# A gated four-branch mixer layer on one core: four small edits around the attention, among them half of the softmax normalisation moved from GpSimd to VectorE

## Chip, cores and metric

The kernel runs on 1 core of a Trainium2 chip. The metric is the device time of one execution in microseconds; the time of a kernel is the median of several runs.

## What is computed

One layer works on a sequence of 1024 tokens with 1024 channels, all in float32. A wide projection of x gives the inputs of four branches; each branch ends in a gated product and a projection, the four results are merged, projected by w_out, added to x and layer-normalised. The change touches the forgetting attention (branch C, 8 heads of 64, causal, query blocks of 128) and the stretch behind it, where the memory cross-attention (branch M) starts. Cut to these:

```python
def _forgetting_attention(q, k, v, logf):
    bsz, seq, heads, dh = q.shape
    scale = dh ** -0.5
    cum = jnp.cumsum(logf, axis=1).transpose(0, 2, 1)
    outs = []
    for i in range(seq // Q_BLOCK):
        q0, end = i * Q_BLOCK, (i + 1) * Q_BLOCK
        s = jnp.einsum('bqhd,bkhd->bhqk', q[:, q0:end], k[:, :end]).astype(jnp.float32) * scale
        decay = cum[:, :, q0:end, None] - cum[:, :, None, :end]
        ...
        s = jnp.where(causal, s + decay, -jnp.inf)
        p = jax.nn.softmax(s, axis=-1).astype(v.dtype)
        outs.append(jnp.einsum('bhqk,bkhd->bqhd', p, v[:, :end]))
    return jnp.concatenate(outs, axis=1)

logf = jax.nn.log_sigmoid((c_f + b_forget[l]).astype(jnp.float32))
o_c = _forgetting_attention(q, k, v, logf).reshape(bsz, seq, C_W)
y_c = (o_c * jax.nn.silu(c_gate)) @ p_c[l]
o_m = _cross_attention(m_q, mk, mv)
y_m = (o_m * jax.nn.silu(m_gate)) @ p_m[l]
```

## The kernel before

Every matrix product of float32 data is made of three matmuls: each operand is split into a rounded high part and the rest (hi and lo), and hi x hi, lo x hi and hi x lo are accumulated. ScalarE makes the high parts, GpSimd or VectorE the low ones by subtraction. The order of each engine's work is written out by hand, and engines are tied together by counting semaphores.

**The stages.** Up to about 590 us TensorE works on the wide projection in pairs of column tiles (`product`, L744 to L746). Then come the first tiles of q, k and v, the forget gates and the memory's k and v (595 to 645 us). The attention runs from there to 943 us in four head pairs c = 0 to 3 (`pair`), then the memory attention together with the branch projections, then w_out and the final layer norm.

**The forget gates.** log sigmoid is made on 8 rows of 1024: ScalarE has |z|, exp(-|z|) (L1339) and ln u (L1341) with u = 1 + exp(-|z|); VectorE corrects ln u by a term with 1/u, a RECIPROCAL (L2024), sums it up (`negcum`) and goes on to k_raw, km_lo, q_stack (`q_lo`) and k_stack_lo (`k_lo`). The sums go to DRAM and come back as `bias`. TensorE's first `scores` wait for k_stack_lo.

**A head pair** has 16 units u (2 heads x 8 query blocks; i = u mod 8; a unit has i + 1 key blocks). For each unit:
- TensorE: `scores` (L899, L901) two units ahead; `turn` transposes the normalised probabilities (L916) into one of two banks of `pt`, in one batch or two; `weigh` (L929), once per two units, multiplies them by v_stack. Between these stands the stream: 64 steps of three matmuls per pair (`stream_part`, L815 to L817), four per unit, which project the next pair's q, k, v and the gate.
- VectorE, iteration k: `biased(k + 1)` adds bias and mask to scores and takes minima (L2085, L2089), `turned_lo(k - 1)` makes pT_lo (L2106), `invert(k + 1)` takes the reciprocal of the row sums (L2099); then, in some iterations, q_lo, k_lo, out_add, gate_half.
- ScalarE: pT_hi (L1394), which in even units waits for the last weigh, exp (L1383), high parts of weights (L1220) and of v (L1412).
- GpSimd, iteration k: `diag_bias(k + 2)` (L1646), `normalise(k + 1)` (L1659) scales the probabilities by the reciprocal, `split_w` for k = 0, 4, 8, 12 (L1622), and for k = 2 in pairs 1 to 3 `z_product` (L1679), the previous pair's o times its gate.

In unit 1 `turn_v` also transposes v (L942: 8 transposes, two batches of 4); the second batch goes into the bank that unit 0 used, and waits for pT_lo of unit 0. The probabilities of unit 1 need the first bank back, so `turn` waits for the low part of v_stack (L2126).

**Behind the last pair** TensorE issues mscores(0) and mscores(1), then for w = 0 to 15 nine steps of M_FILL with the memory attention's transposes in between. The last `weigh(3, 7)` stands behind the first five of these steps. Its result is shifted by ScalarE (L1368), added by VectorE (L2051), and on VectorE follow the row maxima and their negation (L2187, L2190), the memory's normalisation (L2197) and za_lo (L2243), which TensorE needs from step 16 on (L832).

## Time and profile before

| what | value |
|---|---|
| median of 3 runs | 1236.19 us (1235.81 to 1237.3) |
| the profiled execution's own time | 1234.27 us |
| its span | 1232.5 us |
| TensorE matmuls busy | 1202.4 us (98%) |
| VectorE busy | 767.5 us (62%) |
| ScalarE busy | 538.6 us (44%) |
| GpSimd busy | 758.7 us (62%) |
| granted TensorE clock, mean | 0.998 |
| chain that ended last | TensorE 84%, VectorE 8%, GpSimd 3% |

The span runs from the first to the last instruction of one execution; 1.8 us of its time lie outside. A row of the timeline reads: start, duration, engine, line, operation, tile written <- tiles read, shapes, count, and in brackets how long the engine had stood still before it and what ended that. A row of the list of waits reads: total, number of times, longest. In the names of the profile DVE is VectorE, ACT is ScalarE, POOL is GpSimd, PE is TensorE. Rows that merge several instructions overlap their neighbours.

### The profile page before, as it was taken

Reading aid. Unit: us, or ns where it says so; the run is one execution under the profiler, and the core shown is the slowest. Engines: PE = TensorE matmul, PEld = TensorE weight load, DVE = VectorE, ACT = ScalarE, POOL = GpSimd, SP = SyncE. Lnnn points to the kernel's source line nnn. Section 1 sums busy time; section 2 is a strip of 40 time slices with the busy share of each in tenths; the row PEclk is TensorE's granted clock in tenths of the full one; section 3 lists DMA queues with packets and bytes.
Section 4 is the critical chain, followed back from the end, with each engine's and each line's share of the span. In section 5 each row is a group of like instructions: output and inputs, shape, how many; then the busy total and the mean of one; then the engine's idle time right before and its main releaser. Section 6 shows DMA issues by size and latency. Waiting matters only on the chain.

```text
span 1232.5 us, 15758 instructions
## 1 busy us (share of the span) xinstructions
PE 1202.4 (98%) x5704; PEld 998.8 (81%) x5704; DVE 767.5 (62%) x1254; ACT 538.6 (44%) x991; POOL 758.7 (62%) x582
## 2 busy tenths in 40 slices
PE   8999999999999999999999999999999999999997
PEld 6888888888888888888878878878788788878886
DVE  5623865676665755347695564565655776876755
ACT  5433424344434444566344655646555443415000
POOL 6677787877876877877128666677664225557000
PEclk9999999999999999999999999999999999999999
DMA  8012131132332332335222011112002433377141
GB/s 275 9 60 69 35 103 55 66 120 104 102 137 103 103 117 89 137 105 187 87 66 55 24 46 52 35 52 52 18 18 86 165 134 112 111 244 248 63 137 69
DMA packets 91277, 118.61 MB, mean 96 GB/s; under 512 B 6072, under 2 KB 72632, under 8 KB 91200
## 3 DMA queue, kind: packets, MB, share of 16 engines
q1 hardware_dynamic: 91200, 117.60, 29.2%
q8 instruction: 46, 0.75, 0.3%
q14 instruction: 31, 0.25, 0.1%
HBM read 92.39 MB, written 25.20 MB: 95 GB/s over the span
## 4 chain that ended last, share of the span: by engine, by line
PE 84%; DVE 8%; POOL 3%; ACT 2%; issue 2%; DMA 1%; DVEq 0%; SPq 0%; ACTq 0%; POOLq 0%
PE pj L744 11%; PE pj L745 11%; PE pj L746 11%; PE pj L816 4%; PE pj L815 4%; PE pj L817 4%; PE pj L1074 4%; PE pt L745 3%; PE pt L746 3%; PE pt L744 3%; PE po L929 3%; PE pt L916 3%; PE pj L832 2%; PE pj L833 2%; PE pj L834 2%
## 5 line engine op out<-in xcount | busy, mean ns | idle before, releaser
L1569 POOL TENSOR_TENSOR ring_lo<-w_pair,ring_hi 128x512 fp32r<-128x512 f32 x168 | 232.5, 1386 | 110.7 <-ACT ring_hi L1130 110.5
L1622 POOL TENSOR_TENSOR w_lo<-w_raw,w_hi 128x128 fp32r<-128x128 f32 (+1 forms) x104 | 105.1, 1031 | 126.5 <-ACT w_hi L1220 124.4
L1659 POOL TENSOR_SCALAR probs<-probs,rinv 128x128 f32<-128x128 f32 (+3 forms) x64 | 126.4, 1975 | 90.8 <-DVE rinv L2099 90.6
L1130 ACT ACTIVATE ring_hi<-w_pair 128x512 fp32r<-128x512 f32 x168 | 105.1, 628 | 160.6 <-PE pj L746 108.6
L1780 DVE SCALAR_TENSOR_TENSOR po<-glu,cwa,po 128x512 f32<-128x512 f32 x232 | 159.4, 747 | 20.6 <-ACT po L1181 20.6
L744 PE MATMUL pj<-t_hi,ring_hi 128*128 128x512 f32 x392 | 152.8, 390 | 0.3 <-DVE slot L1744 0.3
L745 PE MATMUL pj<-t_lo,ring_hi 128*128 128x512 f32 x392 | 152.5, 389 | 0.0
L746 PE MATMUL pj<-t_hi,ring_lo 128*128 128x512 f32 x392 | 152.5, 389 | 0.0
L815 PE MATMUL pj<-xT_hi,w_hi 128*128 128x512 f32 x320 | 126.0, 394 | 0.0
L816 PE MATMUL pj<-xT_lo,w_hi 128*128 128x512 f32 x320 | 125.5, 392 | 0.0
L817 PE MATMUL pj<-xT_hi,w_lo 128*128 128x512 f32 x320 | 125.1, 391 | 0.0
L1744 DVE TENSOR_TENSOR slot<-pj,copy_p 128x512 f32<-128x512 f32 x56 | 38.5, 688 | 85.6 <-PE pj L746 85.4
L744 PE MATMUL pj<-xT_hi,ring_hi 128*128 128x512 f32 x224 | 87.1, 389 | 0.0
L745 PE MATMUL pj<-xT_lo,ring_hi 128*128 128x512 f32 x224 | 87.1, 389 | 0.0
L746 PE MATMUL pj<-xT_hi,ring_lo 128*128 128x512 f32 x224 | 87.1, 389 | 0.0
L744 PEld LDWEIGHTS pj<-t_hi,ring_hi 128*128 128x128 f32 x392 | 73.6, 188 | 16.5 <-DVE slot L1744 1.3
L746 PEld LDWEIGHTS pj<-t_hi,ring_lo 128*128 128x128 f32 x392 | 73.6, 188 | 15.3
L745 PEld LDWEIGHTS pj<-t_lo,ring_hi 128*128 128x128 f32 x392 | 73.6, 188 | 15.1
L1593 POOL TENSOR_TENSOR w_pair<-w_pair 128x512 f32<-128x512 f32 x56 | 81.8, 1461 | 6.2
L2106 DVE TENSOR_TENSOR pT_lo<-pt,pT_hi 128x512 fp32r<-128x512 f32 (+2 forms) x96 | 50.4, 553 | 53.5 <-ACT pT_hi L1394 53.5
L1744 DVE TENSOR_TENSOR slot<-pt,copy_p 128x512 f32<-128x512 f32 x28 | 19.4, 692 | 96.6 <-PE pt L746 96.6
L1138 ACT ACTIVATE copy_p<-pj 128x512 f32<-128x512 f32 x70 | 41.8, 597 | 81.3 <-PE pj L746 81.3
(343 smaller groups left out, 2939.1 us busy)
## 6 DMA issues: line engine op xcount, KB each, us to landing
w_pair<-in_w_in SPq DMA_DIRECT2D x28, 1024.0 KB, 5.3
gate_scratch<-slot SPq DMA_DIRECT2D x16, 1024.0 KB, 4.0
gate<-gate_scratch SPq DMA_DIRECT2D x32, 512.0 KB, 3.8
w_raw<-in_w_in SPq DMA_DIRECT2D x20, 512.0 KB, 3.9
z_scratch<-slot SPq DMA_DIRECT2D x8, 512.0 KB, 2.6
bias<-cum_scratch SPq DMA_DIRECT2D x8, 512.0 KB, 4.2
wout_raw<-in_w_out SPq DMA_DIRECT2D x8, 512.0 KB, 5.7
x_tok<-in_x SPq DMA_DIRECT2D x8, 512.0 KB, 4.4
```

The costliest lines, as they stand in the source:

```text
L744: nc.tensor.matmul(dst, w_h, hi, start=k == 0 and p in (1, 2, 5), stop=False, skip_group_check=True)
L745: nc.tensor.matmul(dst, w_h, lo, start=False, stop=False, skip_group_check=True)
L746: mm = nc.tensor.matmul(dst, w_l, hi, start=False, stop=k == KH - 1, skip_group_check=True)
L815: nc.tensor.matmul(pj[:, bank, :], w_hi[:, j % 2, k, :], hi, start=k == 0, stop=False)
L816: nc.tensor.matmul(pj[:, bank, :], w_hi[:, j % 2, k, :], lo, start=False, stop=False)
L817: mm = nc.tensor.matmul(pj[:, bank, :], w_lo[:, j % 2, k, :], hi, start=False, stop=k == nk - 1)
L1130: nc.scalar.activation(ring_hi[:, j % RING, :, :], w_src(u, p), ACT.Copy).then_inc(s_rhi, 1)
L1569: nc.gpsimd.tensor_tensor(ring_lo[:, j % RING, :, :], w_src(u, p), ring_hi[:, j % RING, :, :], ALU.subtract).then_inc(s_rlo, 1)
L1593: nc.gpsimd.tensor_tensor(dst, in0, in1, op).then_inc(s_sadd, 1)
L1622: nc.gpsimd.tensor_tensor(w_lo[:, j % 2, k, :], w_raw[:, j % 2, k, :], w_hi[:, j % 2, k, :], ALU.subtract).then_inc(s_wlo, 1)
L1659: nc.gpsimd.tensor_scalar(probs[:, u % 2, 0:(i + 1) * P], probs[:, u % 2, 0:(i + 1) * P], rinv[:, u % 2, 0:1], None, ALU.mult).then_inc(s_ ...
L1780: nc.vector.scalar_tensor_tensor(out=acc if n < PAD_A else src, in0=src, scalar=cwa[:, ct, n:n + 1], in1=acc, op0=ALU.mult, op1=ALU.add).t ...
```

## The change

Four edits. (1) ScalarE makes 1/u as exp(-ln u); VectorE's reciprocal goes, and the counts of that chain's semaphores with it. (2) In unit 1 of each pair `turn_v` stands ahead of the unit's stream steps, and three steps instead of two stand ahead of `turn`. (3) `weigh(3, 7)` stands ahead of the first five M_FILL steps. (4) `normalise` on GpSimd returns for odd units; VectorE scales them inside `invert`, behind its own reciprocal, with a semaphore of its own.

```diff
-        s_pn = sem("probs_normalised")
+        s_pn = sem("probs_normalised_even")
+        s_pnv = sem("probs_normalised_odd")
...
-        F_STEPS = 9
+        F_STEPS = 8
...
-                pe.wait_ge(s_pn, UNITS * c + u + 1)
+                pe.wait_ge((s_pn, s_pnv)[u % 2], NT * c + u // 2 + 1)
...
-                    cut = 4 * u + (3 if u == 0 else 2)
+                    cut = 4 * u + (3 if u < 2 else 2)
+                    if u == 1:
+                        turn_v(c)
                     stream_part(s + S_C, S_C, 4 * u, cut)
                     if u == 0 and c:
                         weigh(c - 1, UNITS // 2 - 1)
-                    if u == 1:
-                        turn_v(c)
                     turn(c, u)
...
+            weigh(CT - 1, UNITS // 2 - 1)
             for w in range(2 * NT):
 
                 m_fill(PER * w, PER * w + 5)
-                if w == 0:
-                    weigh(CT - 1, UNITS // 2 - 1)
-                pe.wait_ge(s_pn, UN + w + 1)
+                pe.wait_ge(s_pn, UN // 2 + w + 1)
...
             nc.scalar.activation(f_l[:, :], f_u[:, :], ACT.Ln).then_inc(s_fa, 1)
+            act.wait_ge(s_fa, 6)
+            nc.scalar.activation(f_r[:, :], f_l[:, :], ACT.Exp, scale=-1.0).then_inc(s_fa, 1)
             split_w(1, 0)
...
             def normalise(c, u):
                 un, i = UNITS * c, u % NT
+                if u % 2:
+                    return
                 pool.wait_ge(s_ri, un + u + 1)
...
-            nc.vector.reciprocal(f_r[:, :], f_u[:, :]).then_inc(s_fv, 1)
-            dve.wait_ge(s_fv, 4)
+            dve.wait_ge(s_fv, 3)
+            dve.wait_ge(s_fa, 7)
...
                 nc.vector.reciprocal(rinv[:, u % 2, 0:1], rsum[:, u % 2, 0:1]).then_inc(s_ri, 1)
+                if u % 2:
+                    i = u % NT
+                    dve.wait_ge(s_ri, un + u + 1)
+                    nc.vector.tensor_scalar(probs[:, 1, 0:(i + 1) * P], probs[:, 1, 0:(i + 1) * P],
+                                            rinv[:, 1, 0:1], None, ALU.mult).then_inc(s_pnv, 1)
```

What this does to the order of instructions shows best at three places. On TensorE, in unit 1 of head pair 1, before:

```order
L815 MATMUL pj<-xT_hi,w_hi 128x512
L816 MATMUL pj<-xT_lo,w_hi 128x512
L817 MATMUL pj<-xT_hi,w_lo 128x512
L942 MATMUL pt<-ident,v_raw 128x128 x8
L916 MATMUL pt<-ident,probs 128x128 x2
```

and now, from the v transposes on (lines stand one further down):

```order
L943 MATMUL pt<-ident,v_raw 128x128 x8
L816 MATMUL pj<-xT_hi,w_hi 128x512
L817 MATMUL pj<-xT_lo,w_hi 128x512
L818 MATMUL pj<-xT_hi,w_lo 128x512
L816 MATMUL pj<-xT_hi,w_hi 128x512
L817 MATMUL pj<-xT_lo,w_hi 128x512
L818 MATMUL pj<-xT_hi,w_lo 128x512
L816 MATMUL pj<-xT_hi,w_hi 128x512
L817 MATMUL pj<-xT_lo,w_hi 128x512
L818 MATMUL pj<-xT_hi,w_lo 128x512
L917 MATMUL pt<-ident,probs 128x128 x2
```

Three steps now stand between v's transposes and those of unit 1's probabilities, where none stood. On GpSimd, units 2 to 5 of head pair 1 (384 to 768 columns), before:

```order
L1659 TENSOR_SCALAR probs<-probs,rinv 128x384
L1646 TENSOR_TENSOR bdiag<-bias,maskc 128x128
L1659 TENSOR_SCALAR probs<-probs,rinv 128x512
L1679 TENSOR_TENSOR z_raw<-z_raw,sg 128x1024
L1646 TENSOR_TENSOR bdiag<-bias,maskc 128x128
L1659 TENSOR_SCALAR probs<-probs,rinv 128x640
L1646 TENSOR_TENSOR bdiag<-bias,maskc 128x128
L1659 TENSOR_SCALAR probs<-probs,rinv 128x768
```

and now:

```order
L1664 TENSOR_SCALAR probs<-probs,rinv 128x384
L1648 TENSOR_TENSOR bdiag<-bias,maskc 128x128
L1684 TENSOR_TENSOR z_raw<-z_raw,sg 128x1024
L1648 TENSOR_TENSOR bdiag<-bias,maskc 128x128
L1664 TENSOR_SCALAR probs<-probs,rinv 128x640
L1648 TENSOR_TENSOR bdiag<-bias,maskc 128x128
L1624 TENSOR_TENSOR w_lo<-w_raw,w_hi 128x256
```

The scalings of 512 and 768 columns are gone, and the z product follows that of 384. On ScalarE, in the forget gates, now:

```order
L1339 ACT_TABLE_LOAD
L1339 ACTIVATE f_e<-f_abs 8x1024
L1341 ACT_TABLE_LOAD
L1341 ACTIVATE f_l<-f_u 8x1024
L1343 ACT_TABLE_LOAD
L1343 ACTIVATE f_r<-f_l 8x1024
L1220 ACTIVATE w_hi<-w_raw 128x256
```

A third table load stands ahead of the new exponential; the load that stood ahead of the attention's first exponential (L1383) is no longer there.

## Rows read from the trace of the kernel before

**Rows 1.** Page, busy time of the engines.
```profile
PE 1202.4 (98%) x5704; PEld 998.8 (81%) x5704; DVE 767.5 (62%) x1254; ACT 538.6 (44%) x991; POOL 758.7 (62%) x582
```

**Rows 2.** TensorE's waits over the whole span: total, times, longest.
```profile
PE pt L916 <- DVE v_stack L2126: 4.3, 4, 1.1
PE pt L916 <- DVE pT_lo L2106: 2.9, 16, 0.2
PE pt L916 <- POOL probs L1659: 2.8, 3, 1.0
PE pj L899 <- DVE k_stack_lo L2069: 2.6, 1, 2.6
PE po L832 <- DVE za_lo L2243: 2.2, 2, 1.8
```

**Rows 3.** Timeline of ScalarE, VectorE and TensorE, 610 to 645 us.
```profile
610.82 1.28 ACT L1341 ACT_TABLE_LOAD   x1
619.20 1.06 ACT L1341 ACTIVATE f_l<-f_u 8x1024 f32<-8x1024 f32 x1 [7.10 <-DVE f_u L2019]
620.34 6.53 DVE L2024 RECIPROCAL f_r<-f_u 8x1024 f32<-8x1024 f32 x1
...
640.81 1.65 DVE L2069 TENSOR_TENSOR k_stack_lo<-k_raw,k_stack_hi 64x1024 fp32r<-64x1024 f32 x1
642.51 0.39 PE L899 MATMUL pj<-k_stack_hi,q_stack 128*128 128x256 f32 x1 [2.63 <-DVE k_stack_lo L2069]
```

**Rows 4.** Timeline of VectorE and TensorE, unit 1 of pair 1.
```profile
723.71 0.28 DVE L2106 TENSOR_TENSOR pT_lo<-pt,pT_hi 128x128 fp32r<-128x128 f32 x1
723.74 0.39 PE L815 MATMUL pj<-xT_hi,w_hi 128*128 128x512 f32 x1
...
724.43 1.03 PE L942 MATMUL pt<-ident,v_raw 128*128 128x128 f32 x8
726.53 0.41 PE L916 MATMUL pt<-ident,probs 128*128 128x128 f32 x2 [1.07 <-DVE v_stack L2126]
```

**Rows 5.** Timeline of GpSimd, VectorE, TensorE: units 3, 4 of pair 1; last row unit 12.
```profile
730.95 2.59 POOL L1659 TENSOR_SCALAR probs<-probs,rinv 128x512 f32<-128x512 f32 x1 [1.81 <-DVE rinv L2099]
733.51 2.40 POOL L1679 TENSOR_TENSOR z_raw<-z_raw,sg 128x1024 f32<-128x1024 f32 x1
734.47 0.17 DVE L2099 RECIPROCAL rinv<-rsum 128x1 f32<-128x1 f32 x1 [0.25 <-ACT probs L1383]
739.22 0.77 PE L916 MATMUL pt<-ident,probs 128*128 128x128 f32 x5 [0.95 <-POOL probs L1659]
771.77 2.77 POOL L1659 TENSOR_SCALAR probs<-probs,rinv 128x640 f32<-128x640 f32 x1 [2.18 <-DVE rinv L2099]
```

**Rows 6.** Timeline of VectorE, TensorE and ScalarE behind the last pair.
```profile
942.54 1.29 DVE L2106 TENSOR_TENSOR pT_lo<-pt,pT_hi 128x512 fp32r<-128x512 f32 x2
943.61 0.28 PE L1019 MATMUL pj<-km_lo,q_stack 128*128 128x256 f32 x1
946.09 0.20 ACT L1467 ACTIVATION_READ_ACCUMULATOR probs<-pj,rmin 128x1 f32 x1
949.27 0.38 ACT L1368 ACTIVATE otmp<-po 64x256 f32<-64x256 f32 x1 [2.98 <-PE po L929]
950.86 1.76 DVE L2190 TENSOR_SCALAR rmin<-rmin 128x2 f32<-128x2 f32 x1
```

**Rows 7.** Single lines: duration in ns min/median/max, first and last start.
```profile
L1998 DVE TENSOR_SCALAR mem_sb<-mem_sb,mv,rinv x2: 807/811/815, 599.1 to 599.8; 128x1024 f32<-128x1024 f32 x2
L2197 DVE TENSOR_SCALAR probs<-probs,rinv x32: 343/354/1197, 946.5 to 1062.0; 128x256 f32<-128x256 f32 x32
L2069 DVE TENSOR_TENSOR k_stack_lo<-k_raw,k_stack_hi x16: 1196/1220/2324, 638.7 to 884.8; 64x1024 fp32r<-64x1024 f32 x16
```

**Rows 8.** VectorE's wait for pT_hi in the attention, 640 to 960 us; its shortest.
```profile
DVE pT_lo L2106 <- ACT pT_hi L1394: 53.5, 31, 3.0
...
779.77 0.89 DVE L2106 TENSOR_TENSOR pT_lo<-pt,pT_hi 128x512 fp32r<-128x512 f32 x2 [1.36 <-ACT pT_hi L1394]
```

More of the change, by code:

```diff
@@ L2023, in _ @@
                                            op0=ALU.subtract, op1=ALU.subtract).then_inc(s_fv, 1)
-            nc.vector.reciprocal(f_r[:, :], f_u[:, :]).then_inc(s_fv, 1)
-            dve.wait_ge(s_fv, 4)
+            dve.wait_ge(s_fv, 3)
+            dve.wait_ge(s_fa, 7)
             nc.vector.scalar_tensor_tensor(out=f_e[:, :], in0=f_e[:, :], scalar=-1.0, in1=f_r[:, :],
                                            op0=ALU.mult, op1=ALU.mult).then_inc(s_fv, 1)
-            dve.wait_ge(s_fa, 6)
-            dve.wait_ge(s_fv, 5)
+            dve.wait_ge(s_fv, 4)
             nc.vector.tensor_tensor(f_l[:, :], f_l[:, :], f_e[:, :], ALU.add).then_inc(s_fv, 1)
             nc.vector.tensor_scalar(f_z[:, :], f_z[:, :], -1.0, 0.0, ALU.mult, ALU.max).then_inc(s_fv, 1)
-            dve.wait_ge(s_fv, 7)
+            dve.wait_ge(s_fv, 6)
             nc.vector.tensor_tensor(f_l[:, :], f_l[:, :], f_z[:, :], ALU.add).then_inc(s_fv, 1)
             dve.wait_ge(s_fone, 1)
-            dve.wait_ge(s_fv, 8)
+            dve.wait_ge(s_fv, 7)
             nc.vector.tensor_tensor_scan(negcum[:, :], f_one[:, :], f_l[:, :], 0.0, ALU.mult,
```

## Prediction

> **What bounds the kernel now.** I read the page first: TensorE is busy for 1202.4 of 1232.5 us [rows 1]. So only time in which TensorE stands still can be won, and that is 30.1 us: a lead before the first matmul, a tail after the last one, and the waits between. Next came TensorE's list of waits [rows 2]: 4.3 us for the v stack (4 times), 2.8 us for GpSimd's normalised probabilities (3 times), 2.6 us once for the k stack, 2.2 us for za_lo (2 times), and 2.9 us in 16 small pieces for pT_lo; apart from the lead the list has nothing else above 0.6 us. Then the timeline around each of the first four places [rows 3 to 6] shows what ended last there. VectorE is not the bound: in the attention it waits 53.5 us for pT_hi alone, 31 times [rows 8]. New VectorE work fits in there if it falls at the right moments.
>
> **Repair 1, the reciprocal.** The 8x1024 reciprocal takes 6.53 us, in a chain in which VectorE never rests until k_stack_lo, 1.65 us from 640.81; TensorE starts its first score matmul at 642.51, after a wait of 2.63 us [rows 3]. The change has ScalarE make 1/u as exp(-ln u). The order of instructions shows a table load between the two (the load that stood before the first softmax exponential is gone for it). ln runs from 619.20 for 1.06 us, the load is 1.28 us like the earlier one, exp is 1.06 us like ln, both 8x1024: f_r is there at 619.20 + 1.06 + 1.28 + 1.06 = 622.60 instead of 620.34 + 6.53 = 626.87, which is 4.27 us earlier [rows 3]. VectorE's chain moves by that, and ScalarE (2.34 us more work, under the memory projections) may hold some of it back; 2.63 us is all that TensorE can take, since its own stream then reaches the scores first. Gain 2.6 us; bounds 1.9 us (4.27 less 2.34) and 2.6 us. I take the upper end, because ScalarE waits for TensorE in between and catches up.
>
> **Repair 2, v turned one step earlier.** In unit 1 of each of the four head pairs TensorE issues 8 transposes of v, then waits 1.07 us until VectorE has made v_stack's low part [rows 2, 4]. A stream step is 0.69 us (723.74 to 724.43 in rows 4). The change issues the v transposes right after the first step instead of the third, and has three steps between them and the probabilities' transposes: 2.07 us of cover where there was none. The old wait goes. But the second four v transposes reuse the bank of unit 0, so they need pT_lo of unit 0, done at 723.71 + 0.28 = 723.99 [rows 4]. TensorE would now be there at 724.43 - 2 x 0.69 + half of 1.03 = 723.57. New wait 0.4 us in pairs 1 to 3; in pair 0, where pT_lo was held up by GpSimd's normalisation of unit 1 and is no more, 0.1 us. Gain 4 x 1.07 - 3 x 0.4 - 0.1 = 3.0 us; bounds 1.0 us (if pT_lo is 0.4 us later everywhere, the new wait is 0.8 us) and 4.3 us.
>
> **The normalisation.** GpSimd loses 32 TENSOR_SCALARs, VectorE gets them. Two rows bound their price: 128x256 takes 354 ns, 128x1024 takes 811 ns [rows 7]. With 0.50 and 0.66 us for 512 and 768 columns the eight of a pair cost 2 x (0.35 + 0.50 + 0.66 + 0.81) = 4.6 us, 18.6 us in all. All of that stands behind a reciprocal and ahead of the next unit's bias step on VectorE. I put it on the path with 0 us in the units where VectorE waits for pT_hi next, since the least wait I found ahead of a unit with two batches is 1.36 us [rows 8].
> What it gives: in unit 4 of pairs 1 to 3 TensorE waits 0.95 us [rows 5]. There GpSimd did normalise(3) (2.59 us), z_product (2.40 us), a diagonal and then normalise(4). Without normalise(3) the z product starts up to 2.6 us earlier and is out of the way. Then normalise(4) hangs on its reciprocal: 734.47 + 0.17, plus 2.77 us (its duration when VectorE's k_stack_lo runs beside it, row of 771.77), is 737.4 [rows 5]. TensorE without its wait is there at 739.22 - 0.95 = 738.27, and by repair 2 some 0.65 us earlier, 737.6. The new normalise(3) on VectorE, 0.50 us, stands ahead of that reciprocal. So 0.3 us of wait stays: gain 3 x (0.95 - 0.3) = 2.0 us, bounds 0 and 2.85 us.
> What speaks against it: VectorE is held up by a running GpSimd instruction. A 128x256 scaling took 1197 ns instead of 354 beside GpSimd's split of weights, k_stack_lo took 2324 instead of 1220 ns beside the z product [rows 7], and the 128x2 negation took 1.76 us [rows 6]. The new instruction can be caught by what GpSimd still runs in such a unit: the z product (unit 3, pairs 1 to 3) or a split of weights (units 1, 5, 9 and 13). At the least this costs nothing, where VectorE starts first. At the most it is 2.4 us in one unit (z product, rows 5), less the 1.36 us of rest. I charge 0.1 us a pair and 0.1 us for the z products, 0.5 us together, near the lower end because of the rests in rows 8. The Trainium skill, "SBUF — State Buffer", section "SBUF: two separate sides", speaks against this edit: the two engines share a port pair by an exclusive lock, and the later one waits for the whole instruction of the other. The durations named agree with it; taken for every scaling that meets a split it gives rival D, 1240.2 us, where the rests of rows 8 give 1227.1 us.
>
> **Repair 3, the last weigh.** weigh(3, 7) now runs ahead of five stream steps (3.4 us). It needs the last pT_lo, done at 942.54 + 1.29 = 943.83; TensorE ends the memory scores' issue at about 943.7 (0.12 us behind the matmul of 943.61), so 0.15 us of wait is new [rows 6]. After it stands a single chain: o shifted (949.27), added, row maxima, negation (1.76 us beside the z product, as it will be again), exponential, normalisation, za_lo, for whose third and fourth blocks TensorE waits 2.2 us [rows 2, 6]. weigh now ends 3.3 us earlier, but ScalarE reads the sum of its first memory exponential until 946.29 [rows 6], so the shift starts at 946.3 and the chain moves by 2.5 us or more, which covers the 2.2 us. Gain 2.2 - 0.15 - 0.1 (the fourth block) = 1.95 us; bounds 0 and 2.2 us.
>
> **Sum.** 2.6 + 3.0 + 2.0 - 0.5 + 1.95 = 9.05 us. The profiled execution took 1234.27 us; against its own time that gives 1225.2 us. The median of the three runs is 1.9 us above that execution, and the forecast is for a median: 1236.19 - 9.05 = 1227.1 us. What lies behind this stretch is bound by TensorE and moves as a whole.
>
> **Rivals.**
> A. As above, 1227.1 us; own range 1224.8 to 1229.0. Chance 0.66.
> B. Port trouble and late reciprocals eat part: the wait in unit 4 stays at 0.95 us and each pair loses a further 0.7 us where a scaling stands behind a GpSimd instruction. 9.05 - 2.0 - 2.8 = 4.25 us, 1231.9 us. For it: the longest durations [rows 7]. Against: VectorE's rests [rows 8]. Chance 0.20.
> C. The change does not do what it says: v's transposes only trade one wait for another, since pT_lo of unit 0 is late (repair 2 gives its lower bound, 1.0 us). 1227.1 + 2.0 = 1229.1 us. For it: pT_lo ends 0.4 us behind TensorE already in this trace [rows 4]. Chance 0.08.
> D. Slower. The scaling meets GpSimd's split of weights and delays pT_lo of the even unit before it. In units 5 and 13 of each pair, 8 places, such a split follows on GpSimd, and TensorE already waits 0.18 us for exactly that pT_lo (16 pieces in rows 2, units 7 and 15 are the other 8), so only VectorE's rest of 1.36 us stands between a late VectorE and TensorE. With a scaling of 0.66 us and 2.4 us of blocking each place loses 0.66 + 2.4 - 1.36 = 1.7 us: 1236.19 - 9.55 + 8 x 1.7 = 1240.2 us. It decides from 9.55 / 8 = 1.2 us a place. For it: the longest scaling, 1197 ns [rows 7]. Against: that one lost 0.84 us, not 2.4. Chance 0.04.
> E. The change is worth more than the waits: the small waits of 0.18 us vanish as well, and repair 2 gives its 4.3 us. 1224 us or a little under. Chance 0.02.
>
> **How the numbers follow.** About 0.2%, 2.5 us, is what a measurement of this kernel can tell from no change. A, C and E are faster by more; of B (4.25 us) all but 0.04, of D nothing. Faster 0.92, within 0.2% 0.04, slower 0.04. The range takes A with the bounds of its unknown terms, C, and about half of B: 1224.3 to 1231.5 us.
>
> **What would show it.** Right: TensorE's wait for k_stack_lo gone and an exp of 8x1024 at about 621.6; v_stack gone from TensorE's waits and a wait of about 0.4 us ahead of the second four v transposes; the wait for GpSimd's probs at 0 to 0.4 us a pair; za_lo nearly gone; VectorE's scaling at 0.35 to 0.81 us, GpSimd with 32 scalings fewer. Wrong: scalings on VectorE of 1.5 us and more with a longer wait of TensorE for pT_lo behind them, or a first score matmul that still waits.

## The result, and the profile after

The changed kernel takes 1223.22 us (median of 5, 1221.87 to 1224.24) against 1236.19 us (median of 5 of the kernel before): ratio 0.9895, 95% interval 0.9881 to 0.9909. That is 13.0 us less, where 9.05 were forecast; the time lies 1.1 us under the low end of the range. The profiled execution took 1223.87 us with a span of 1222.1 us, 10.4 us less than that of before in both.

The page and TensorE's list of waits after the change:

```profile
PE 1203.0 (98%) x5704; PEld 999.2 (82%) x5704; DVE 781.5 (64%) x1285; ACT 539.5 (44%) x992; POOL 693.5 (57%) x550
...
L1664 POOL TENSOR_SCALAR probs<-probs,rinv 128x128 f32<-128x128 f32 (+3 forms) x32 | 57.9, 1810 | 110.8 <-DVE rinv L2103 110.8
...
L2115 DVE TENSOR_TENSOR pT_lo<-pt,pT_hi 128x512 fp32r<-128x512 f32 (+2 forms) x96 | 50.4, 553 | 48.4 <-ACT pT_hi L1396 48.4
```

```profile
PE pj L770 <- ACT ring_hi L1236: 6.4, 1, 6.4
PE pt L917 <- DVE pT_lo L2115: 2.9, 16, 0.2
PE pt L943 <- DVE pT_lo L2115: 0.9, 3, 0.3
PE pj L833 <- DVE gate L2243: 0.5, 2, 0.3
PE pj L833 <- DVE zb_lo L2286: 0.4, 2, 0.2
```

TensorE's work is what it was [rows 1]. Four of the five waits of [rows 2] are gone: v_stack, GpSimd's probs, k_stack_lo and za_lo. The 16 small ones for pT_lo are untouched, and one is new: 0.28 us, three times, ahead of v's second four transposes (L943).

Timeline of ScalarE, VectorE, GpSimd and TensorE at the forget gate (answers to [rows 3]). The exponential comes in at 622.88, VectorE stands still 2.32 us for it, and yet TensorE starts its first score matmul with no wait in the list:

```profile
621.59 1.28 ACT L1343 ACT_TABLE_LOAD   x1
622.88 1.06 ACT L1343 ACTIVATE f_r<-f_l 8x1024 f32<-8x1024 f32 x1
624.05 1.21 DVE L2031 SCALAR_TENSOR_TENSOR f_e<-f_e,f_r 8x1024 f32<-8x1024 f32 x1 [2.32 <-ACT f_r L1343]
624.39 4.21 POOL L1624 TENSOR_TENSOR w_lo<-w_raw,w_hi 128x256 fp32r<-128x256 f32 x2 [28.34 <-ACT w_hi L1220]
625.29 1.63 DVE L2034 TENSOR_TENSOR f_l<-f_l,f_e 8x1024 f32<-8x1024 f32 x1
626.86 2.29 DVE L2035 TENSOR_SCALAR f_z<-f_z 8x1024 f32<-8x1024 f32 x1
...
639.92 1.22 DVE L2073 TENSOR_TENSOR k_stack_lo<-k_raw,k_stack_hi 64x1024 fp32r<-64x1024 f32 x1
640.59 0.39 PE L817 MATMUL pj<-xT_lo,w_hi 128*128 128x512 f32 x1
640.82 0.39 PE L818 MATMUL pj<-xT_hi,w_lo 128*128 128x512 f32 x1
641.20 0.39 PE L900 MATMUL pj<-k_stack_hi,q_stack 128*128 128x256 f32 x1
```

The same two VectorE instructions, f_l and f_z, in the kernel before:

```profile
628.22 1.22 DVE L2030 TENSOR_TENSOR f_l<-f_l,f_e 8x1024 f32<-8x1024 f32 x1
629.36 0.67 DVE L2031 TENSOR_SCALAR f_z<-f_z 8x1024 f32<-8x1024 f32 x1
```

They take 2.0 us more now, beside GpSimd's split of weights (624.39, rough as GpSimd's spans are), which before stood beside the reciprocal (620.71, 2.50 us). And k_stack_lo is still what TensorE's first score comes for last: it ends at 641.14, the score starts at 641.20, 0.38 us behind the matmul ahead of it, where neighbouring matmuls start 0.23 us apart. About 0.15 us is lost there that no list of waits shows.

Timeline of units 1 to 4 of pair 1 (answers to [rows 4, 5]):

```profile
721.16 0.29 DVE L2115 TENSOR_TENSOR pT_lo<-pt,pT_hi 128x128 fp32r<-128x128 f32 x1 [0.20 <-ACT pT_hi L1396]
721.51 0.66 PE L943 MATMUL pt<-ident,v_raw 128*128 128x128 f32 x4 [0.28 <-DVE pT_lo L2115]
722.25 1.29 DVE L2135 TENSOR_TENSOR v_stack<-pt,v_stack 128x512 fp32r<-128x512 f32 x2 [0.79 <-ACT v_stack L1414]
724.09 0.38 PE L917 MATMUL pt<-ident,probs 128*128 128x128 f32 x2
...
725.64 2.40 POOL L1684 TENSOR_TENSOR z_raw<-z_raw,sg 128x1024 f32<-128x1024 f32 x1
...
727.43 0.90 DVE L2107 TENSOR_SCALAR probs<-probs,rinv 128x512 f32<-128x512 f32 x1
...
731.85 0.16 DVE L2103 RECIPROCAL rinv<-rsum 128x1 f32<-128x1 f32 x1 [0.52 <-ACT probs L1385]
732.04 1.22 DVE L2073 TENSOR_TENSOR k_stack_lo<-k_raw,k_stack_hi 64x1024 fp32r<-64x1024 f32 x1
732.11 2.91 POOL L1664 TENSOR_SCALAR probs<-probs,rinv 128x640 f32<-128x640 f32 x1 [3.46 <-DVE rinv L2103]
734.76 0.39 PE L818 MATMUL pj<-xT_hi,w_lo 128*128 128x512 f32 x1
735.07 0.77 PE L917 MATMUL pt<-ident,probs 128*128 128x128 f32 x5
```

v_stack's low part, two instructions, now ends at 723.54, 0.55 us ahead of the transposes. Before, the second of the two ended at 726.98, 0.45 us behind their start. The z product starts at 725.64, well clear of unit 4. normalise(4) hangs on its reciprocal and ends at 732.11 + 2.91 = 735.02, and TensorE starts its transposes at 735.07. That is no slack: the start is 0.31 us behind the matmul of 734.76, where 0.23 us would do, so normalise(4) still ends last, with 0.08 us that the list of waits does not show. Part of what GpSimd gave up was also a collision. k_stack_lo behind that reciprocal took 2.32 us beside the z product before, and takes 1.22 us now. (In each of pairs 0 to 2 the next pair's k_stack_lo of unit 13 is longer instead, 1.64 and not 1.22 us, beside a split of weights.)

**Where the time went.** From TensorE's timeline I summed every stand-still of over 0.1 us between its first and its last matmul: 16.6 us before, 5.2 us after, 11.4 us less. By stretch: 2.63 us ahead of the first score, 10.00 to 3.69 us in the four pairs, 2.43 to 0.14 us from there to the first zb matmul. The rest hardly moved. The last matmul ends at 1214.60 instead of 1225.03. The trace of after had lost 1.3 us already when it came to the slot wait near 566 us, in code that no edit touches (lead 0.36 us longer, then 559.98 instead of 559.02 us); this stretch takes 559.0 to 560.3 us in the traces of this study, with no kernel the better for it.

**What a stand-still costs beyond its length.** The profile counts a stand-still from the modelled end of the matmul ahead of it. A matmul of 512 columns has a row of 0.39 us, but the next one starts 0.23 us behind it when nothing holds it up (640.59 and 640.82 above). A stand-still of 0.18 us is therefore a step of 0.57 us in place of 0.23: 0.34 us lost. Each of them costs about 0.16 us more than its listed length, and one of up to 0.16 us is not listed at all. The wait of 0.15 us that the forecast had for repair 3 is one of these. The last pT_lo ends at 936.15, and the weigh behind it starts at 936.20, 0.28 us behind the matmul ahead of it instead of 0.12:

```profile
935.80 0.28 PE L1019 MATMUL pj<-km_hi,q_stack 128*128 128x256 f32 x1
935.92 0.28 PE L1020 MATMUL pj<-km_lo,q_stack 128*128 128x256 f32 x1
936.20 0.38 PE L930 MATMUL po<-pT_hi,v_stack 128*128 128x256 f32 x1
```

Counted from start to start, TensorE's way from the matmul ahead of the first score to the last matmul is 11.8 us shorter after the change: 2.6 us at the first score, 6.4 us in the four pairs, 2.6 us from there to the first zb matmul and 0.15 us behind it.

The 13.0 us of the medians are 1.2 us more than those 11.8 us. The interval of the ratio, 11.2 to 14.7 us, is wide enough to hold both; experiments 9, 10, 13 and 14 look for what else it can be.

### The profile page after: what moved, and what is told of

The parts are those of the page before. It is cut to its first block, busy times and chain, and to the rows that moved or that the text cites. A ratio compares the mean times of both kernels' runs of the same rounds, so it can differ in the third digit from the quotient of the medians.

```text
span 1222.1 us, 15758 instructions
## 1 busy us (share of the span) xinstructions
PE 1203.0 (98%) x5704; PEld 999.2 (82%) x5704; DVE 781.5 (64%) x1285; ACT 539.5 (44%) x992; POOL 693.5 (57%) x550
## 4 chain that ended last, share of the span: by engine, by line
PE 86%; DVE 7%; ACT 3%; issue 2%; DMA 1%; POOL 1%; DVEq 0%; SPq 0%; ACTq 0%
PE pj L745 11%; PE pj L746 11%; PE pj L747 11%; PE pj L816 5%; PE pj L817 5%; PE pj L818 5%; PE pj L1074 4%; PE pt L746 3%; PE pt L747 3%; PE pt L745 3%; PE po L930 3%; PE pt L917 2%; PE po L1074 2%; PE pt L1074 2%; PE pj L833 2%
## 5 line engine op out<-in xcount | busy, mean ns | idle before, releaser
L1624 POOL TENSOR_TENSOR w_lo<-w_raw,w_hi 128x128 fp32r<-128x128 f32 (+1 forms) x104 | 111.2, 1088 | 161.6 <-ACT w_hi L1220 159.5
L1664 POOL TENSOR_SCALAR probs<-probs,rinv 128x128 f32<-128x128 f32 (+3 forms) x32 | 57.9, 1810 | 110.8 <-DVE rinv L2103 110.8
L1396 ACT ACTIVATE pT_hi<-pt 128x512 fp32r<-128x512 f32 (+2 forms) x96 | 43.7, 489 | 77.4 <-PE po L930 67.8
```

The source lines that it names most:

```text
L1624: nc.gpsimd.tensor_tensor(w_lo[:, j % 2, k, :], w_raw[:, j % 2, k, :], w_hi[:, j % 2, k, :], ALU.subtract).then_inc(s_wlo, 1)
```

## The experiments

Each was timed against the kernel before on the same chip, whose medians were 1236.14 us (experiments 1 to 4), 1234.70 (5 to 8), 1236.24 (9 to 12) and 1236.16 us (13, 14). "Stand-still" is the sum described above, 16.6 us in the first trace of before, without the 0.16 us that each one costs on top. The ratio on record is not the quotient of the two medians; the two can differ by 0.0011, 1.3 us (experiment 9), and where they differ the interval is the safer guide.

| experiment | median us | ratio, 95% interval | stand-still less by, us |
|---|---|---|---|
| 1 reciprocal only | 1232.33 | 0.9970 (0.9959 to 0.9981) | 2.5 |
| 2 v turn only | 1233.90 | 0.9988 (0.9979 to 0.9997) | 2.7 |
| 3 last weigh only | 1232.99 | 0.9973 (0.9964 to 0.9982) | 1.9 |
| 4 normalisation only | 1233.47 | 0.9982 (0.9973 to 0.9991) | 2.2 |
| 5 the three repairs | 1227.70 | 0.9941 (0.9928 to 0.9953) | 7.3 |
| 6 all units on VectorE | 1225.40 | 0.9926 (0.9913 to 0.9938) | 10.1 |
| 7 odd units scaled twice | 1230.95 | 0.9969 (0.9957 to 0.9981) | 4.2 |
| 8 later turns | 1223.16 | 0.9903 (0.9889 to 0.9916) | 10.2 |
| 9 change without repair 1 | 1225.99 | 0.9928 (0.9914 to 0.9941) | 8.4 |
| 10 the change again | 1223.25 | 0.9903 (0.9888 to 0.9917) | 11.7 |
| 11 v turn in two | 1223.41 | 0.9901 (0.9889 to 0.9914) | 10.9 |
| 12 v in two, later turns | 1222.10 | 0.9891 (0.9879 to 0.9904) | 12.0 |
| 13 longer stand-still | 1234.26 | 0.9984 (0.9975 to 0.9993) | 1.9 |
| 14 the kernel before again | 1235.42 | 0.9992 (0.9983 to 1.0001) | 0.6 |

### 1 to 4: each edit alone

Each takes the hunks of one edit from the diff above. Their first lines, in order:

```diff
+            nc.scalar.activation(f_r[:, :], f_l[:, :], ACT.Exp, scale=-1.0).then_inc(s_fa, 1)
-            nc.vector.reciprocal(f_r[:, :], f_u[:, :]).then_inc(s_fv, 1)
```
```diff
-                    cut = 4 * u + (3 if u == 0 else 2)
+                    cut = 4 * u + (3 if u < 2 else 2)
+                    if u == 1:
+                        turn_v(c)
```
```diff
+            weigh(CT - 1, UNITS // 2 - 1)
             for w in range(2 * NT):
```
```diff
+                if u % 2:
+                    return
                 pool.wait_ge(s_ri, un + u + 1)
```

> Only edit 1 (1/u by ScalarE). Theory T1 (the four edits act at separate waits of TensorE and add up; the rest of the measured gain is the spread of the stage before 566 us): the wait of 2.63 us for k_stack_lo goes to 0, nothing else moves, 2.6 us faster than before. Theory T2 (the edits help one another, or move other work than the waits forecast): clearly more than 2.6 us, or 0 to 1 us alone.

> Only edit 2 (v transposed two steps earlier, three steps ahead of the probabilities). T1: the four waits of 1.07 us for v_stack go, new waits for pT_lo of unit 0 come. In pair 0 GpSimd's normalisation of unit 1 still stands ahead of the diagonal, so the new wait there is about 1 us; in pairs 1 to 3 it is 0.3 to 0.5 us. Gain 1.8 to 2.5 us, less than the 3.4 us that the full change shows. T2: the full 3.4 us or more.

> Only edit 3 (the last weigh ahead of five stream steps). T1: the waits for za_lo (2.2 us) and the one for merged (0.2 us) go, a wait of 0.15 us comes: 2.2 us faster. T2: 0 to 1 us, since the chain is held by the z product on GpSimd.

> Only edit 4 (odd units scaled by VectorE). T1: the three waits of 0.95 us for GpSimd's probabilities go whole, no new wait of TensorE comes: 2.85 us faster. The forecast had 2.0 us with 0.3 us of wait left a pair, and 0.5 us of port trouble. T2 (the port trouble is real and hidden only by the other edits): under 1.5 us, with TensorE's waits for pT_lo longer than 0.18 us.

Waits of TensorE in the traces of the v turn alone and of the normalisation alone:

```profile
PE pt L916 <- POOL probs L1659: 2.8, 3, 0.9
PE pj L899 <- DVE k_stack_lo L2069: 2.6, 1, 2.6
PE po L832 <- DVE za_lo L2243: 2.2, 2, 1.8
PE pt L942 <- DVE pT_lo L2106: 2.0, 4, 0.8
```
```profile
PE pt L917 <- DVE v_stack L2134: 4.3, 4, 1.1
...
PE pt L917 <- POOL probs L1662: 0.7, 3, 0.3
```

The reciprocal alone takes its 2.63 us whole (the start of the first score still comes 0.41 us behind the matmul ahead of it, not 0.23). The v turn alone trades 4.3 us for 2.0 us: 0.81 us in pair 0, where pT_lo is held up by GpSimd's normalise(1), and 0.40 us in the others, the number that I had worked out. The normalisation alone leaves 0.25 us in unit 4 of pairs 1 to 3. That is near the forecast 0.3 us, but not by its working, which had those 0.3 us only together with repair 2 and nothing without it (normalise(4) done at 737.41 + 0.50, TensorE there at 738.27). What made the wait is port trouble: in unit 3 the scaling takes 0.90 instead of 0.50 us and k_stack_lo behind it 1.37 instead of 1.22 us, and normalise(4) takes 2.91 instead of 2.77 us. The weigh alone takes the 2.2 us of za_lo and adds the 0.15 us that I had forecast, unlisted: its first matmul starts 0.28 us behind the one ahead of it, not 0.12 us. So alone, each edit gives about what its step said. The sum of the four differences of medians is 3.8 + 2.2 + 3.2 + 2.7 = 11.9 us; each has an interval of about 1 us to either side, so it can't tell adding up from helping one another. The traces can: edits 2 and 4 help each other (experiment 5).

### 5 to 8: together, more on VectorE, and later turns

```diff
 # 5: edits 1, 2 and 3 without edit 4
 # 6, against the change: even units on VectorE too (and normalise on GpSimd returns at once)
-                if u % 2:
+                if True:
 # 7, against the change: odd units scaled a second time, by 1.0
+                    nc.vector.tensor_scalar(probs[:, 1, 0:(i + 1) * P], probs[:, 1, 0:(i + 1) * P],
+                                            1.0, None, ALU.mult).then_inc(s_pnv, 1)
 # 8, against the change
-                    cut = 4 * u + (3 if u < 2 else 2)
+                    cut = 4 * u + (3 if u < 2 or u % NT in (5, 7) else 2)
```

> Edits 1, 2 and 3 without the move of the scalings. T1 (parts add up): the three waits of 0.95 us for GpSimd's probabilities stay, v's transposes in pair 0 wait about 1 us more than in the full change: 7.3 to 8.0 us faster than before, some 3.5 us slower than the full change. T2 (the move hurts elsewhere and the repairs carry all): as fast as the full change or faster.

> All four edits, and the even units' scalings on VectorE too, some 18 us more on VectorE in all. T1 (VectorE's rests while it waits for pT_hi and for scores hide the scalings): within 1.5 us of the full change. Rival D of the prediction (pT_lo of even units is pushed by scalings ahead of it): the 16 waits of 0.18 us grow to 0.5 us and more each, over 5 us slower than the full change.

> All four edits; VectorE scales each odd unit a second time, by 1.0: 32 instructions of 0.35 to 0.81 us more and a semaphore each, some 20 us of new VectorE work at the very place of the moved scalings. T1: hidden but for unit 12 of each pair, where the rest before pT_lo was 1.36 us and would now be about 0: 0 to 2 us slower than the full change. Rival D: every odd scaling counts, 5 to 20 us slower.

> All four edits, and in units 5, 7, 13 and 15 three stream steps instead of two ahead of the transposes, one behind. If the 16 waits of 0.18 us for pT_lo are the latency from the last weigh over pT_hi and pT_lo, a step more covers them: 2.9 us faster than the full change, unless the scores, now a step later, or GpSimd's scaling of units 6 and 14 (0.4 to 1.2 us of slack, a step is 0.69 us) end last there and give 0.3 us a pair back.

**5.** Without the normalisation the three waits for GpSimd's probs stay at 0.91 us and v's wait is 0.93 us in pair 0 and 0.39 us in the others. With it they are 0, 0 and 0.28 us. So edit 4 is worth 2.7 + 0.9 + 0.3 = 3.9 us of stand-still on top of the repairs (4.5 us by the medians), but 2.2 us by itself. Timelines say why. In experiment 4 VectorE reaches the reciprocal of unit 4 at 735.90 and TensorE its transposes at 738.88 (they start at 739.13); normalise(4) takes 2.91 us between the two and 0.25 us is missing. With repair 2 VectorE is done with v_stack about 1 us earlier against TensorE's transposes, so its whole chain of units 2 to 4 comes earlier too: in the change the two times are 731.85 and 735.07. In both cases TensorE starts 3.2 us behind the reciprocal, as soon as normalise(4) is done; what became shorter is how long it had stood ready.

**6.** The even units on VectorE too bring nothing. TensorE now waits 0.52 us in unit 4 of pairs 1 to 3 for pT_lo, its list has 4.6 us for pT_lo where the change has 2.9 us, and its own work in the four pairs is 1.2 us longer (306.9 instead of 305.7 us). That is no slower work but the hidden part of the same waits: step by step against the change, 2.8 us are lost in one kind of place, the fifth and last transpose of units 4 and 12, which waits for pT_lo, and the matmul behind it. There a transpose has a row of 0.27 us and the next starts 0.11 us behind it when it is free to; now steps of 0.25 to 0.79 us stand there. 2.2 us slower than the change by the medians, where up to 1.5 us were expected of theory T1 and over 5 us of rival D.

**7.** A second scaling of the odd units adds 5.2 us to the list's pT_lo, and nearly all of it in one place: unit 13 of pairs 0, 1 and 2. The VectorE and TensorE rows there of the change, and then of the kernel that scales twice with the GpSimd row beside them:

```profile
698.33 0.62 DVE L2107 TENSOR_SCALAR probs<-probs,rinv 128x768 f32<-128x768 f32 x1
698.98 1.64 DVE L2073 TENSOR_TENSOR k_stack_lo<-k_raw,k_stack_hi 64x1024 fp32r<-64x1024 f32 x1
...
702.29 0.89 DVE L2115 TENSOR_TENSOR pT_lo<-pt,pT_hi 128x512 fp32r<-128x512 f32 x2 [0.28 <-ACT pT_hi L1396]
703.13 0.85 PE L917 MATMUL pt<-ident,probs 128*128 128x128 f32 x6 [0.18 <-DVE pT_lo L2115]
```
```profile
698.46 3.19 POOL L1625 TENSOR_TENSOR w_lo<-w_raw,w_hi 128x256 fp32r<-128x256 f32 x2 [0.98 <-ACT w_hi L1221]
698.97 0.98 DVE L2111 TENSOR_SCALAR probs<-probs 128x768 f32<-128x768 f32 x1
699.98 2.76 DVE L2074 TENSOR_TENSOR k_stack_lo<-k_raw,k_stack_hi 64x1024 fp32r<-64x1024 f32 x1
...
704.04 0.88 DVE L2119 TENSOR_TENSOR pT_lo<-pt,pT_hi 128x512 fp32r<-128x512 f32 x2
704.88 0.85 PE L918 MATMUL pt<-ident,probs 128*128 128x128 f32 x6 [1.94 <-DVE pT_lo L2119]
```

The median is 7.7 us above the change, where T1 had 0 to 2 us and rival D 5 to 20 us: D's size, but not by its reason that every odd scaling counts. For those three places this is rival D's mechanism. The second scaling costs 0.98 us and pushes k_stack_lo to where it is held up beside GpSimd's split of weights, 2.76 us instead of 1.64 us. That is 2.1 us more on VectorE against a rest of 0.28 us, and TensorE's wait goes from 0.18 to 1.94 us. The Trainium skill, "SBUF — State Buffer", section "SBUF: two separate sides", has the two engines exclude each other on a shared pair of ports, and these rows agree with it in kind: 2.76 us beside GpSimd, 1.22 us alone. The rest of 1.36 us in [rows 8] was this very place (pair 1, the third unit from the end). In the change the scaling with its issue took 0.65 us of it, and k_stack_lo, already 1.64 instead of 1.22 us beside the split, another 0.42 us: 0.28 us are left. In pair 3, where no k_stack_lo follows, even the doubled scaling leaves a rest of 1.10 us. The trace has a smaller loss too: three waits of 0.39 us for GpSimd's probs in unit 4.

**8.** TensorE waits 0.18 us in units 5, 7, 13 and 15 for pT_lo. One more stream step ahead of those transposes takes these 16 waits, but 8 of 0.24 us come behind units 5 and 13, v's wait in the next pair rises from 0.28 to 0.67 us, and the last weigh waits 0.38 us. Stand-still in the pairs: 4.28 us instead of 3.69 us. The 2.9 us were not there to be had by moving one step; the wait moved on with it. The pairs are still 0.8 us shorter, since TensorE's own time in them is 1.4 us less. Nearly all of this, 1.25 us, is at the steps from a stream matmul to the transposes: eight waits are gone, and each had cost 0.16 us beyond its 0.18. The median, 1223.16 us, is that of the change.

### 9 to 12: taking repair 1 back out, and two versions more

```diff
 # 9: edits 2, 3 and 4 without edit 1;  10: the change itself
 # 11, against the change
                     if u == 1:
-                        turn_v(c)
-                    stream_part(s + S_C, S_C, 4 * u, cut)
+                        turn_v(c, 0)
+                        stream_part(s + S_C, S_C, 4 * u, 4 * u + 1)
+                        turn_v(c, 1)
+                    stream_part(s + S_C, S_C, 4 * u + (u == 1), cut)
 # 12: 11 with the cut of 8
```

> All of the change but repair 1, so TensorE should again stand still for 2.6 us ahead of the first score matmul. Theory: that stand-still costs more than its length, because in a part of the executions the granted clock falls to 0.50 for some 3 us right behind it, as it did in the profile of the v turn alone (644.0 to 647.2 us). Then the mean granted clock is 0.997 or lower in about half of the executions, and the median is 3.5 to 5 us above that of the whole change, near 1227.5. Rival: the stand-still costs its length and nothing else; then the median is 2.6 us above the whole change, 1225.9, and its spread is like that one's (2.4 us between the lowest and the highest).

> The changed kernel itself, for a comparison on one chip. Its trace took 11.3 us of stand-still from TensorE (lead not counted) and its median is 13.0 us below. Theory: the difference is the clock behind the stand-still of 2.6 us, which about half of the executions of the kernel before have and which this one does not have: 1223.2 us again, ratio 0.989 to 0.9905, clock 0.998 or 0.999 in nearly all executions, and the executions of the kernel before at 0.998 or more lie 11 to 12 us above it. Rival: the 13.0 us were spread of the untouched first stage; then the ratio comes back to 0.991 (11.3 us).

> The changed kernel with v's second four transposes issued one stream step behind the first four, in unit 1 of each pair. In the trace of the change TensorE waits 0.28 us for pT_lo between them in pairs 1 to 3; one step is 0.69 us. By the waits it gains 3 x 0.28 = 0.8 us, unless v_stack's low part comes late in its turn, since only two steps are left behind the second four: then the old v_stack wait comes back in part (up to 0.4 us a pair) and the gain is nothing or a loss of 0.8 us.

> The same with the probabilities' transposes of units 5, 7, 13 and 15 one stream step later as well. In the trace of that edit alone TensorE's waits of 0.18 us for pT_lo went from 16 to 8 of 0.24, but the wait between v's two halves rose from 0.28 to 0.67 us, because pT_lo of unit 0 of the next pair came later. With v in two that wait has 0.69 us of cover: 3 x 0.67 = 2.0 us less than the later turns alone, about 1221.5 us. If the gain is only moved on again, to the waits behind unit 1, it comes out at 1223 us.

**10** repeats the time: 1223.25 us, all four executions at a mean granted clock of 0.998 or 0.999. Its median is 13.0 us below that of before, its ratio of 0.9903 says 12.0 us (10.3 to 13.8), and so it doesn't tell the theory's 13 us from the rival's 11.3 us. The theory's other sign came: the five executions of the kernel before at 0.998 or more have a median of 1234.28 us, 11.0 us above the change. **9** is 2.7 us above it, the price of the wait alone, and its theory asked for 3.5 to 5 us. (The wait's length is 2.63 us, its cost from start to start 2.8 us less the 0.15 us that stay in the change.) One of its six executions had a clock of 0.996 and took 1229.72 us, the others 0.998 or more. So the median spoke for the rival and one execution for the theory: undecided, and the reason for experiments 13 and 14.

**11.** v's wait is gone, but GpSimd's probs in unit 4 are waited for again, 1.4 us in three pieces, in place of 0.9 us: VectorE's v_stack takes 1.47 instead of 1.29 us, now that its second part waits for a later transpose, and unit 4, where the change had nothing to spare, pays for it. No gain, by a road that I had not named. **12** is the best of all, 1222.10 us, 1.15 us under the change on the same chip; the two intervals overlap, so this is a hint only. Its trace has 0.3 us less stand-still than that of 10. It lies between the 1221.5 us expected and the 1223 us of a gain only moved on; part was moved on, to unit 4 (0.45 us, three times) and the last weigh (0.38 us).

### 13 and 14: the clock behind a stand-still

```diff
 # 13, against experiment 9
-            nc.vector.reciprocal(f_r[:, :], f_u[:, :]).then_inc(s_fv, 1)
+            nc.vector.reciprocal(f_r[:, :], f_u[:, :]).then_inc(s_r1, 1)
+            dve.wait_ge(s_r1, 1)
+            nc.vector.reciprocal(f_r[:, :], f_u[:, :]).then_inc(s_fv, 1)
 # 14: the kernel before
```

> The change without repair 1, with the reciprocal made twice, so that TensorE stands still for about 2.6 + 6.5 = 9.1 us ahead of the first score matmul. Theory: the clock falls behind a stand-still, the longer the surer. Then the profile shows a granted clock of 0.50 for some us behind the stand-still, nearly every execution has a mean granted clock of 0.997 or less, and the median is above 1225.99 + 6.5 = 1232.5 by the price of the low clock, 1.5 us or more. Rival: the low clock in the profile of the v turn alone came by chance and has nothing to do with the stand-still; then the median is 1232.5 and the clocks are spread as before, 0.998 in most.

> The kernel before, for one more profile of it. If the 2 us by which its median lies above its first profiled execution are the low clock behind the stand-still, then the granted clock in 642 to 660 us tells with the time: either 0.50 for some 3 us there and a time near 1236, or 1.00 and a time near 1234. If such an execution has its low clock elsewhere, or none and still takes 1236, the theory falls.

Windows of TensorE's timeline: us, TensorE busy, granted clock, DMA share, GB/s. First the v turn alone, behind its wait of 2.6 us that ends at 642.47; then experiment 14, at its two waits for za_lo (1.78 us until 963.22 and 0.33 us until 964.62); then experiment 13, behind 9.18 us of stand-still:

```profile
642.50:644.00 1.50, 1.50 (x7) 0.97 0.00 0
644.00:647.00 3.00, 3.00 (x8) 0.50 0.56 132
647.00:650.00 3.00, 3.00 (x16) 0.94 0.17 49
```
```profile
958.00:963.50 5.50, 3.72 (x20) 1.00 0.16 47
963.50:967.00 3.50, 3.18 (x9) 0.56 0.00 0
967.00:970.00 3.00, 3.00 (x16) 0.94 0.17 31
```
```profile
641.00:645.50 4.50, 0.00 (x0) 0.98 0.38 89
645.50:655.00 9.50, 4.96 (x13) 0.50 0.61 184
655.00:660.00 5.00, 5.00 (x26) 0.94 0.00 0
```

The profiled execution of experiment 14 took 1236.2 us and its low clock lies behind the za_lo waits, not in 642 to 660 us. So by its own words the theory of experiment 14 falls in the form that I had given it, with the k stack's wait as the only cause. What replaces it is wider, and was made up after the fact: the fall can come behind either of the two longest stand-stills. Experiment 9 had kept one of them only.

The clock goes to 0.50, the lower of its two levels, 1.2 GHz, and back. In the v turn alone matmuls of 512 columns then start 0.43 us apart instead of 0.23, and the stretch from the first score to the first v transpose lasts 8.15 us instead of the 6.55 us that the same 31 matmuls take in the change: 1.6 us lost. In experiment 13 it lasts 9.13 us: 2.6 us lost. There the fall comes inside the stand-still already, near 645 us, and its median of 1234.26 us is 1.8 us above the 1232.5 us of the length alone, as its theory had asked (1.5 us or more). In experiment 14 the loss is 1.0 us (55.2 us of work from the za to the zb matmuls, 54.2 before). The first trace of before has the same stand-stills and no fall. So whether one comes behind 2 or 3 us of stand-still differs from execution to execution; behind 9 us it came in all 11. In the other executions only the mean granted clock is on record. It can stand for a fall: the three traces with a fall have means of 0.997, 0.997 and 0.994, and the thirteen without one, the first of before among them, 0.998 or 0.999. By this sign the executions sort by the stand-stills that their kernel keeps:

| kernels | longest stand-stills kept | clock 0.997 or less |
|---|---|---|
| the kernel before, experiments 2, 4 | 2.6 us (k stack), 2.2 us (za_lo) | 70 of 104 |
| experiments 1, 3, 9 | one of the two | 5 of 23 |
| experiment 7 | three of 1.9 us | 3 of 6 |
| the change, experiments 5, 6, 8, 10, 11, 12 | none over 1 us | 0 of 31 |
| experiment 13 | 9.2 us | 11 of 11 |

And of the kernel before alone, 82 executions: median 1234.4 us for the 27 with a clock of 0.998 or more, 1236.1 us for the 34 with 0.997, 1237.0 us for the 21 with less. Over all of them it is 1236.1 us. Taken as cause, the fall of the clock is worth 1.7 us of the kernel's median. That is read from a sorting and not from an edit: no run takes the fall away and leaves the stand-stills. Nor is its share steady, 23 of 29, 16 of 21, 6 of 11 and 3 of 10 executions in the four sets; in the last, against which experiments 5 to 8 were timed, the median of before is 1234.70 us.

## Why the prediction was wrong

The direction and the places were right, and so were the mechanisms of the repairs as a whole, though two numbers came out by luck (see repair 1 and the normalisation). What was wrong is the size: 3.9 us between the forecast of 1227.1 us and 1223.22 us. Two steps failed. The larger part, 2.7 us, lies in the terms: 9.05 us were forecast, and 11.8 us went from TensorE's way. With 11.8 us the forecast would have been 1224.4 us, just inside the range. The rest, 1.2 us, took the time out of it.

**The level of the median, 1.2 us.** The step that failed is in the part on the sum: "The median of the three runs is 1.9 us above that execution, and the forecast is for a median: 1236.19 - 9.05". I took the 1.9 us for a constant between a profiled execution and a median, and carried it over. The change has no such offset: its profiled execution lies 0.65 us above its median. The likely cause is the clock behind two stand-stills that the change removes, worth 1.7 us of the median of before by the clocks of 82 executions; a part of the 1.9 us is the first stage, which in that one trace of before was the shortest of all (559.0 us). I counted a stand-still at its listed length; by these runs it costs that length, 0.16 us on top, and, in a part of the executions, the low clock behind it. Against the profiled execution the sum gave 1225.2 us, and 1223.87 us came, but the closeness is luck: that trace lost 1.3 us in the untouched first stage. The Trainium skill, "TensorE: Matmul & The Clock Gate", section "What's actually happening", says of the slow matmuls when activity starts that their number varies from run to run, and that their price is under 1% of a typical kernel's span, not to be fitted in a model. The first agrees in kind with what was seen here in mid-kernel (70 of 104 executions), the second in size (1.7 of 1236 us), and yet the price is as large as a term of this sum.

**The terms, 2.7 us.** In the whole change, by TensorE's timelines, as stand-still and from start to start:

| term | forecast | stand-still | start to start |
|---|---|---|---|
| repair 1 | 2.6 | 2.6 | 2.6 |
| repair 2 | 3.0 | 4.3 - 3 x 0.28 = 3.4 | 3.2 |
| normalisation, unit 4 | 2.0 | 2.85 | 3.05 |
| trouble at the ports | -0.5 | 0 | 0 |
| repair 3 | 1.95 | 2.3 | 2.6 |
| sum | 9.05 | 11.2 | 11.5 |

The 0.3 us between 11.5 and 11.8 are pieces of a few hundredths spread over the other units and the end.

- Repair 1: the right number, by luck. The step "VectorE's chain moves by that" (4.27 us) failed. f_r is there 3.43 us behind the start of ln instead of 7.67 us, 4.2 us earlier; but the chain to the end of k_stack_lo takes 20.63 us instead of 23.26 us (620.51 to 641.14, before 619.20 to 642.46), only 2.63 us less. f_l and f_z lose 2.0 us beside GpSimd's split of weights, and k_stack_lo gets 0.4 us back (1.22 instead of 1.65 us). What was left happened to be TensorE's wait of 2.63 us, to within the 0.15 us named above.
- Repair 2: 0.4 us a pair was right as long as GpSimd scaled (0.39 us in experiment 5). With the scaling gone from GpSimd its next diagonal is early, VectorE waits 0.78 us for TensorE instead of 1.58 us for that diagonal, and pT_lo comes 0.1 us earlier: 0.28 us. Pair 0 has no wait, where I had 0.1 us.
- Normalisation, the largest miss of a term: the step "TensorE without its wait is there at 739.22 - 0.95 = 738.27, and by repair 2 some 0.65 us earlier" failed. It moved TensorE forward and left the reciprocal behind normalise(4) where it was. Repair 2 moved VectorE's chain as well, and of the remaining 0.25 us of experiment 4 (0.41 us from start to start) 0.08 us are left.
- Ports: the scalings cost VectorE 20.9 us instead of 18.6 us, so they were caught at times (0.90 us in unit 3, beside the z product). Within the change TensorE paid next to nothing for it (in experiment 4 it paid the 0.25 us), and a larger collision went at the same time: k_stack_lo, 2.32 to 1.22 us. The dearest collision of all, the 2.0 us on repair 1's chain, no term had looked for. I had looked only for what a scaling runs into, not for what a shorter list on GpSimd no longer runs into.
- Repair 3: the new wait of 0.15 us for the last pT_lo came, below what the list shows (0.28 instead of 0.12 us from start to start). But the 0.2 us for merged went too, and each wait that went had cost 0.16 us beyond its length, so the stretch is 2.6 us shorter.

Of the rivals, B did not happen, and C only in small: in pair 0 of experiment 2. D's mechanism is real and has its place in unit 13, not in units 5 and 13 of every pair; experiment 7 shows it, 0.28 us further on. E, over the waits by the small pieces of 0.18 us, was the wrong reason for the right side: all 16 pieces are still there. The low end of the range, 1224.3 us, is the upper bounds of all terms together (2.6 + 4.3 + 2.85 + 2.2 = 11.95, which gives 1224.2 us). The terms came near them; for the level of the median the range had left nothing.

## What to carry to other kernels

When you take a stand-still out of a kernel that is bound by TensorE, look at the granted clock of many executions, not of the one with a profile: the wait costs its length and, sometimes, half the clock for some us behind it. Cost a wait from start to start of the matmuls around it, not by its listed length, and when a term comes out right, check that its chain moved as you said. Don't carry the distance between a profiled execution and the median over to the changed kernel. Where two edits shift the same engine's chain, cost the second against the chain as the first leaves it; and where work leaves GpSimd, look for VectorE instructions that stood beside it, as well as for those that the new work will stand beside.

## What was not expected of the hardware

- Behind 2.6 us, and behind 2.2 us, of a standing TensorE the granted clock fell to 0.50 for about 3 us in one trace each. By the mean granted clock (0.997 or less) such a fall came in 70 of 104 executions with both stand-stills in the kernel, in 5 of 23 with one, and in 0 of 31 with none over 1 us. With 9.2 us of stand-still it came in 11 of 11; in the trace the clock was back only after 655 us, over 5 us after the matmuls had begun again.
- A stand-still of TensorE in the list costs about 0.16 us more than it says, and one of up to 0.16 us isn't listed: a 512-column matmul has a row of 0.39 us and the next starts after 0.23 us. The 16 waits of 0.18 us for pT_lo that the change leaves are 16 x 0.34 = 5.4 us, not 2.9.
- Two VectorE scalings of the same 128x768 took 0.62 us and, half a microsecond into a GpSimd instruction, 0.98 us; the 64x1024 subtraction behind took 2.76 us instead of 1.22 us. One operand or two, both forms took longer. At the forget gates an 8x1024 scaling took 2.29 us instead of 0.67 beside such a split.
- Where 559 us of TensorE work have no wait in them, their length still differs by 1.3 us between traces of the same instructions. What causes that stays open.
